# Second block of a two-block transformer: sums of a double norm made earlier, a small projection with its weights loaded, an MLP norm beside the output products

## The reference

```python
    h = rmsnorm(h, final_g)          # end of the first model, eps 1e-5
    return h[:, N_META:]
...
    h = rmsnorm_2(x, norm_mix[l])    # start of the second, eps 1e-6
    (dn_qkv, dn_z, dn_b, dn_a, ns_q, ...) = jnp.split(h @ w_in[l], splits, axis=-1)
...
    x = x + mix @ w_out[l]
    h2 = rmsnorm_2(x, norm_mlp[l])
    x = x + jnp.square(jax.nn.relu(h2 @ w_up[l])) @ w_down[l]
```

## Time and profile before

| | us |
|---|---|
| median of 3 runs | 2912.18 |
| lowest, highest | 2909.5, 2913.94 |
| the profiled execution | 2919.71 |
| its span, first to last instruction | 2917.8 |
| PE busy | 2648.9 (91%) |
| POOL busy | 1276.2 (44%) |
| DVE busy | 1204.6 (41%) |
| ACT busy | 980.7 (34%) |
| mean granted clock of PE | 0.941 |

### The profile page before, as it was taken

The page is one execution under the profiler, slowest core; times in us unless marked ns, Lnnn a source line. Parts: engine busy times, 40 slices in busy tenths (PEclk is TensorE's granted clock), DMA queues, the critical chain, the costliest instruction groups (busy, mean ns, idle before and its releaser), DMA issues.

```text
span 2917.8 us, 47590 instructions
## 1 busy us (share of the span) xinstructions
PE 2648.9 (91%) x18844; PEld 2372.1 (81%) x18844; DVE 1204.6 (41%) x1962; ACT 980.7 (34%) x1822; POOL 1276.2 (44%) x602
## 2 busy tenths in 40 slices
PE   5988999998896999999599898899999889699999
PEld 5976999998894999999588687688777777578777
DVE  5965532233776443033448543202555612220210
ACT  3335322223234332222436322233656642221221
POOL 4471665566463366566624310123111155464452
PEclk8988999999897899999789899999999989799999
DMA  4210222222220022221213000322111143132222
GB/s 134 73 59 10 79 86 76 98 75 94 66 84 15 30 96 80 96 88 64 81 44 116 16 2 2 92 67 64 47 43 44 44 154 99 43 101 87 86 87 72
DMA packets 174121, 203.88 MB, mean 70 GB/s; under 512 B 6427, under 2 KB 158582, under 8 KB 173702
## 3 DMA queue, kind: packets, MB, share of 16 engines
q1 hardware_dynamic: 170192, 199.37, 20.8%
q10 hardware_dynamic: 3766, 2.25, 0.3%
HBM read 193.22 MB, written 8.39 MB: 69 GB/s over the span
## 4 chain that ended last, share of the span: by engine, by line
PE 78%; DVE 8%; POOL 4%; issue 4%; ACT 3%; DVEq 2%; DMA 1%; ACTq 0%; POOLq 0%; SPq 0%
PE ps L716 17%; PE ps L717 16%; PE ps L718 16%; PE ps L1551 6%; POOL wlo L2742 2%; PE ps L1441 2%; PE ps L822 2%; PE ps L961 2%; PE ps L1423 1%; DVE conv L2242 1%; DVE gained L2135 1%; PE ps L1386 1%; PE ps L1169 1%; PE ps L1093 1%; DMA wraw<-in_w_proj_dn 1%
## 5 line engine op out<-in xcount | busy, mean ns | idle before, releaser
L2742 POOL TENSOR_TENSOR wlo<-wraw,whi 128x2048 fp32r<-128x2048 f32 x182 | 837.8, 4604 | 1019.3 <-ACT whi L1613 1019.1
L716 PE MATMUL ps<-hn_hi,whi 128*128 128x264 f32 (+1 forms) x2752 | 894.8, 325 | 44.4 <-POOL hn_lo L2869 12.6
L717 PE MATMUL ps<-hn_lo,whi 128*128 128x264 f32 (+1 forms) x2752 | 881.8, 320 | 0.0
L718 PE MATMUL ps<-hn_hi,wlo 128*128 128x264 f32 (+1 forms) x2752 | 879.7, 320 | 0.0
L716 PEld LDWEIGHTS ps<-hn_hi,whi 128*128 128x128 f32 x2752 | 525.5, 191 | 83.7 <-issue 36.6
L718 PEld LDWEIGHTS ps<-hn_hi,wlo 128*128 128x128 f32 x2752 | 524.3, 191 | 36.6
L717 PEld LDWEIGHTS ps<-hn_lo,whi 128*128 128x128 f32 x2752 | 525.5, 191 | 32.4
L1613 ACT CAST whi<-wraw 128x2048 fp32r<-128x2048 f32 x182 | 346.2, 1902 | 587.1 <-PE ps L718 404.1
L716 PE MATMUL ps<-ff_hi,whi 128*128 128x264 f32 x704 | 201.3, 286 | 20.9 <-POOL wlo L2742 11.4
L718 PE MATMUL ps<-ff_hi,wlo 128*128 128x264 f32 x704 | 200.3, 285 | 0.0
L717 PE MATMUL ps<-ff_lo,whi 128*128 128x264 f32 x704 | 199.9, 284 | 0.0
(11 more groups left out here) (454 smaller groups left out, 4366.9 us busy)
## 6 DMA issues: line engine op xcount, KB each, us to landing
wraw<-in_w_in SPq DMA_DIRECT2D x54, 1024.0 KB, 5.1
wraw<-in_w_gate_up SPq DMA_DIRECT2D x44, 1024.0 KB, 5.0
wraw<-in_w_up SPq DMA_DIRECT2D x16, 1024.0 KB, 5.5
wraw<-in_w_down SPq DMA_DIRECT2D x16, 1024.0 KB, 4.7
wraw<-in_w_out SPq DMA_DIRECT2D x12, 1024.0 KB, 5.1
wraw<-in_w_down SPq DMA_DIRECT2D x16, 768.0 KB, 4.5
wraw<-in_w_down SPq DMA_DIRECT2D x16, 640.0 KB, 4.3
gate_dram<-gate_out SPq DMA_DIRECT2D x16, 256.0 KB, 2.1
```

The source lines that it names most:

```text
L716: nc.tensor.matmul(dst, whi[:, slot, c:c + P], rhs_hi, start=start, stop=False)
L717: nc.tensor.matmul(dst, whi[:, slot, c:c + P], rhs_lo, start=False, stop=False)
L718: return nc.tensor.matmul(dst, wlo[:, slot, c:c + P], rhs_hi, start=False, stop=stop)
L2742: nc.gpsimd.tensor_tensor(wlo[:, slot, :], wraw[:, slot, :], whi[:, slot, :].bitcast(F32), ALU.subtract).then_inc(w_split, 1)
```

## The change

- In the last down products ACT also squares gained, and DVE adds these squares into gained_sum. As gained is h times the gain of the final norm, both sums of the double norm exist at the hand-over: sum(h^2) and sum((h g)^2). norm_sums makes eight column sums; DVE works out both scales on four columns, ACT takes one root of eight, and PE spreads two sets of rows. t2 comes straight from h with the product of both gains (mix_cols); x2 is written between the t2 steps.
- The small projection has the 64 weight columns loaded and 512 tokens streaming. It and the first two fills go chunk by chunk, as chunks come. Its result is copied by ACT and turned back by four transposes after the third fill. The gates and g are made between the steps of the first fills, on ACT (small_steps) and DVE (head_gates); the matmuls of g go from behind fill 1 to behind fill 6.
- Attention loop: p_cmp is scaled and shifted on DVE and takes one exponential for four heads, in a step and signal of its own behind the window's; DVE makes its sum. The gate copy goes from ACT to DVE.
- MLP norm: squares on ACT and sums on DVE behind each output fill, four column sums, and the first two up fills go chunk by chunk.

The diff, cut:

```diff
-            def norm2(idx):
-                for i, (ready, n) in enumerate(((sq_pool, idx - M0), (sq_dve, idx + 1))):
...
+            def norm_sums(x, at):
+                for t in range(NT2):
+                    last = nc.tensor.matmul(ps[:, 6, at + t:at + t + 1], x[:, tile(t)], ones[:, 0:1], start=True, stop=True)
+                return last
...
+            norm_sums(square_sum[:, N_META:T1], 0)
+            norm_sums(gained_sum[:, N_META:T1], NT2).then_inc(sums_done, 1)
+            pe.wait_ge(rms_ready, M0 + 1)
+            spread2(rstd, 12, 4).then_inc(rows_ready, 1)
+            spread2(rstd, 8, 5).then_inc(rows_ready, 1)
...
+            for k in range(KD):
+                pe.wait_ge(hn_ready, (M0 + 1) * KD + k + 1)
+                for c in range(2):
+                    last = product(ps[:, c, :], 0, k, c, hx(hn_hi, k, 0, SEQ), hx(hn_lo, k, 0, SEQ), k == 0, k == KD - 1)
...
+                for i, (x, w) in enumerate(((hn_hi, ws_hi), (hn_lo, ws_hi), (hn_hi, ws_lo))):
+                    last = nc.tensor.matmul(ps[0:64, 7, :], w[:, 64 * k:64 * k + 64], hx(x, k, 0, SEQ),
+                                            start=(k == 0 and i == 0), stop=(k == KD - 1 and i == 2))
+            last.then_inc(small_raw_done, 1)
...
+                if c == 2:
+                    small_turned()
+                if c == 3:
+                    pe.wait_ge(x2_ready, KD)
+                if c == 6:
                     pe.wait_ge(g_ready, 1)
...
                 nc.scalar.copy(hn(hn_hi, c, 0, T1), gained[:, c % 4, :]).then_inc(hi_ready, 1)
+                if again:
+                    nc.scalar.activation(gained_sq[:, c % 2, :], gained[:, c % 4, :], ACT.Square)
                 nc.scalar.activation(sq[:, c % 2, 0:T1], h[:, c, :], ACT.Square).then_inc(sq_ready, 1)
...
+            def small_steps(c):
+                if c == 1:
+                    act.wait_ge(small_raw_done, 1)
+                    nc.scalar.copy(small_raw, ps[0:64, 7, :]).then_inc(small_copied, 1)
+                if c == 2:
...
+                    nc.scalar.activation(gates, small[:, :, 16:64], ACT.Sigmoid)
+                    nc.scalar.activation(beta, small[:, :, 0:DN_HEADS], ACT.Sigmoid).then_inc(small_act, 1)
+                if c == 3:
+                    nc.scalar.activation(a_exp[:, 0, :], head_rows[:, 0, :], ACT.Exp)
+                    act.wait_ge(a_abs_ready, 1)
...
+                if part == 2:
+                    p = p_cmp[slot][:, :, 0:N_CMP]
+                    nc.scalar.activation(p, p, ACT.Exp)
...
-            norm2(M0 + 2, lambda c: ((x2_added, c + 1), x2[:, c, :]), eps6, M0 + 2)
+            for f in range(KD):
+                act.wait_ge(x2_added, f + 1)
+                nc.scalar.activation(sq[:, f % 2, 0:SEQ], x2[:, f, :], ACT.Square).then_inc(sq_ready, 1)
+                if f % 2:
+                    follow(PN_WO + f // 2, EV_WO + f + 1)
...
+                    if again:
+                        nc.vector.tensor_tensor(gained_sum, gained_sum, gained_sq[:, c % 2, :], ALU.add)
...
             for u in range(UNITS):
+                if u:
+                    gate_copy(u - 1)
                 if u + 1 < UNITS:
                     scores_in(u + 1)
                 combine(u)
+            gate_copy(UNITS - 1)
...
             for f in range(KD):
                 dve.wait_ge(products_done, E0 + EV_WO + f + 1)
                 nc.vector.tensor_tensor(x2[:, f, :], x2[:, f, :], ps[:, f, :], ALU.add).then_inc(x2_added, 1)
+                dve.drain()
+                if f:
+                    mlp_square(f - 1)
```

More of the change, by code:

```diff
@@ L210, in hybrid_blocks @@
         o_raw = qk_raw
-        sq8 = put("sq8", [P, KD, PADT], work)
         v_at = work + 4 * KD * T1
@@ L1525, in _ @@
                 last.then_inc(products_done, 1)
-            pe.wait_ge(x2_added, KD)
-            norm2(M0 + 2)
+            pe.wait_ge(sq_dve, M0 + 2)
+            norm_sums(mlp_sum, 0).then_inc(sums_done, 1)
+            pe.wait_ge(rms_ready, M0 + 2)
+            spread2(rstd, 8, 4).then_inc(rows_ready, 1)
+            pe.wait_ge(w_split, N0 + PN_UP[0] + 3)
+            for k in range(KD):
+                pe.wait_ge(hn_ready, (M0 + 2) * KD + k + 1)
+                for f in range(2):
+                    last = product(ps[:, f, :], 0, k, f, hx(hn_hi, k, 0, SEQ), hx(hn_lo, k, 0, SEQ), k == 0, k == KD - 1)
+                    if k == KD - 1:
+                        last.then_inc(products_done, 1)
+            pe.wait_ge(w_split, N0 + PN_UP[0] + 4)
+            for f in range(2, 4):
+                pe.wait_ge(relu_sq_ready, f + 1)
+                fill(f, 1, f % 2, hn_hi, hn_lo)
             for part in range(2):
-                with pe.Fori(0, 4) as i:
+                with pe.Fori(1 - part, 4) as i:
                     for f in range(4):
-                        if part == 0 and f == 0:
-                            pe.wait_ge(hn_ready, (M0 + 3) * KD)
                         if f % 2 == 0:
@@ L2102, in _ @@
                     follow(PN_MNS + c // 2, EV_MNS + c + 1)
-            for j in range(4):
-                follow(PN_WO + j, EV_WO + 2 * j + 2)
-            norm2(M0 + 2, lambda c: ((x2_added, c + 1), x2[:, c, :]), eps6, M0 + 2)
+            for f in range(KD):
[3 more added lines that the diff above has]
+                    follow(PN_WO + f // 2, EV_WO + f + 1)
+            act.wait_ge(rstd_ready, M0 + 2)
+            nc.scalar.activation(rstd[:, 8:12], rstd[:, 0:4], ACT.Sqrt).then_inc(rms_ready, 1)
+            split2((M0 + 2) * KD)
             for part in range(2):
@@ L2456, in _ @@
-            for ch in range(2):
-                last = nc.vector.tensor_scalar(g_half[:, ch, :], g_log.rearrange(flat), halves[:, ch:ch + 1], None, ALU.mult)
-            last.then_inc(g_ready, 1)
             nc.vector.memset(state, 0.0).then_inc(state_ready, 2)
@@ L2743, in lower @@
                                         ALU.subtract).then_inc(w_split, 1)
-            def add_squares(idx, n):
-                for c in range(1, KD // 2):
-                    pool.wait_ge(sq_ready, idx * KD + (c + 1))
-                    last = nc.gpsimd.tensor_tensor(sq8[:, 0, 0:n], sq8[:, 0, 0:n], sq8[:, c, 0:n], ALU.add)
-                    if c < KD // 2 - 1:
-                        pool.drain()
-                last.then_inc(sq_pool, 1)
             def chunk_rest(at, c):
```

245 lines of the change are left out of this document (126 added, 119 removed).

## The result

| | median, us | lowest to highest (runs) | before on the same chip | ratio, 95% interval |
|---|---|---|---|---|
| the change | 2867.73 | 2860.08 to 2875.26 (4) | 2912.24 | 0.9847 [0.9827, 0.9866] |
| after_again | 2859.43 | 2858.15 to 2864.59 (5) | 2915.58 | 0.9808 [0.9776, 0.9840] |
| after_third | 2858.39 | 2855.62 to 2861.62 (5) | 2913.23 | 0.9810 [0.9787, 0.9832] |

The first row is the measurement that the forecast was made for; the other two are the same kernel on two other occasions, beside experiments. The change makes the kernel 1.5% faster in the first and 1.9% in the others, 44.5 to 56 us. The forecast was 2861 us, 2850 to 2875. (The ratios are those on record, with their 95% intervals. They are not the quotients of the two medians and differ a little from them, most for no_table_loads: 0.9815 against 0.9795.)

What follows compares the result with a forecast made beforehand. The prediction took TensorE's matmul work as the bound (78% of the chain that ended last). Its terms, 3.3 − 34.4 + 0.6 + 2.6 − 3 − 20.4 = −51.3, took 2919.7 us to 2868.4 profiled, 2861 median, range 2850 to 2875.

Steps and rivals of the forecast that it cites:

- 1. Down products: Down turns of both layers: ACT's extra Square makes PE wait 0.55 us longer six times, +3.3 us.
- 2 and 3. Norm and products at the hand-over: Hand-over to block 2: earlier norm and chunk-paced products end at 1459.1 instead of 1493.54, −34.4 us.
- 4, turning: Behind the third qkv fill: four transposes turn the small product back, about +0.6 us.
- 5, the stall: Behind the fifth qkv fill: PE waits once for ACT, which has table loads and small steps queued, +2.6 us.
- step 3: Products at the hand-over: 72 at 0.229 us each plus a restart of 2.75 us make 19.2 us.
- 6. The attention loop: Attention loop: ACT's saving ends part of PE's long waits, −5; DVE's new work costs some; together −3 us.
- 7. The MLP norm: MLP norm: sums beside the output products and chunk-paced up fills end at 2524.2 instead of 2544.55, −20.4 us.
- the low clock through the chunk-paced fills (2883): Both restarts: clock stays at its lower level while chunks pace PE, 22 us more, 2883 us; chance 0.06.
- the loop paced by DVE (2875): Attention loop: DVE's new work shows in every unit, 11 us instead of −3, 2875 us; chance 0.11.
- no overlap (2881): Hand-over and MLP norm: fills still begin after the last chunk, each place loses about 10 us, 2881 us; chance 0.03.
- the slower case: Block 2's qkv fills: low level lasts through 22 fills, which lose 121 us, 2982 us; chance 0.02.
- Larger gain (2850): Squares hide in PE's waits, ACT does not stall, the loop gives 8: 11 us more, 2850 us; chance 0.10.

Runs made afterwards that it cites:

- no_table_loads: The change with the decay's two exponentials and logarithm in block 2's qkv fills made as Squares, so decays differ from the reference; 2853.66 us, ratio 0.9815.
- mlp_only: The kernel before with only the MLP norm's part of the change; 2890.55 us, ratio 0.9916.
- late_square: The change with ACT's Squares of gained behind the whi cast in each layer's first three down turns, DVE adding them after square_sum; 2861.05 us.
- half_square: The kernel before with an extra ACT Square over 64 of 512 columns in the down turns, result unread; 2913.19 us against 2915.58, ratio 0.9992.

## Why the prediction was right

The forecast (2861 us) lies between the three medians of the change, the sum (−51.3) next to the difference of the two profiles (−52.05). By step:

1. Down products, forecast +3.3. The mechanism I gave is there, 1.9 us a layer or +3.7 in all. What the step did not have is the clock: each wait between 2.3 and 2.9 us can be followed by a stretch at 0.50 that costs 1.45 us. On A and C, the stages of the edit, the first profile shows +12.6, after_again +6.7 and after_third +9.7, so the step was too small by 9.3, 3.4 and 6.4 us. B, which holds no edited product, is +0.6 in the first and −3.3 and −3.6 in the others. Of the 9.6 us between the first profile and after_again 5.9 lie in A and C and 3.9 in B, and of the 7.1 to after_third 2.9 and 4.2. So the first median need not be the highest by this term; the other runs were not traced.

2 and 3. Norm and products at the hand-over, −34.4; 4, turning, +0.6; 5, the stall, +2.6: together −31.2. H went from 223.8 to 193.2, 191.7 and 193.0: −30.6 to −32.1. The restart at the lower level, for which step 3 had 2.75, cost 1.5 us in the first and third, and after_again had none. Inside, the norm took 11.5 us from the last sum to the first product (10.7 forecast; the row of mix_cols can account for up to 0.7 of the 0.8) and the 72 products 18.4 (19.2). The stall was 2.92 (2.6), for the reason given: without the loads, or with one fill more between, it goes. Each load was followed at once by its function here too, so the 4.1 us that the Trainium skill's rule ("ScalarE: Activation LUTs", What ACT_TABLE_LOAD costs) would have added did not come.

6. The attention loop, −3 with bounds of −8 and +8. As an edit to before it gave −4, in the change −17 us by the medians and −14.6 by the two profiles. The step counted ACT's saving at the long waits (−5; the waits went down by 6.1) and charged DVE's new work 2 us that never showed: against traces without a long low stretch L falls by 7.7. The step missed that before's loop had two low stretches behind these waits, 6.8 us, which no trace with the new loop has. They stand in the trace of before (its mean level over the loop is 0.96), but none of my groups asked what the level did there.

7. The MLP norm, −20.4: M went from 282.6 to 262.7, −19.9, and mlp_only gave −21.8.

So the sum was right by terms 2 to 5 and 7 (−51.6 together, −50.5 in the first profile) and, in the first profile, by two errors of opposite sign, the clock's share in both left out: 9.9 us too little cost over A, B and C, 11.6 us too small a gain in step 6. That they cancel is luck. In the two later jobs the gain was 56.2 and 54.8 us, 3.5 to 5 more than the sum. Of the rivals, the low clock through the chunk-paced fills (2883) fell with the row at 1458.04, the loop paced by DVE (2875) with the 7.7 us, no overlap (2881) with the first product at 1454.21, while the last t is made from 1461.05, and the slower case with the level of 1.00 from 1458 to 1493. Larger gain (2850) had three conditions: the loop nearly met its own (7.7 of 8), but ACT did stall, 2.92 us, and the Squares did not hide.

## What to carry to other kernels

A norm between two products costs PE little of its own and much in standing still: make its sums beside the products that feed it, and let the next products start with the first finished chunk. Where they then start at the low clock, work that is paced but dense can still bring the level back, as it did here at both restarts, after 3.2 and 5.9 us.

When an operation is put on the queue of an engine that PE waits for, add to the wait what the clock may take behind it. Waits of 1.6 to 2.9 us could be enough for it here. The 20 small ones in the loop lost 6.1 us in sum, and the medians moved by 4 us in one kernel and by 17 in the other.

Look at what POOL does when DVE's new operation will start. Here adds of 0.71 us took 4.6 to 5.0 us where they started inside a subtraction on POOL, and late_square, which took the Squares out of ACT's way, gained nothing.

Compare a variant with its parent on one chip and in one job. The 6.7 us that late_square seemed to give were the difference between two measurements of the parent.

## What the runs showed that I had not expected

PE's level falls to 0.50 after waits of 1.6 to 2.9 us in the middle of dense work, but not after each of them: 2.53 us in half_square was followed by a low stretch in layer 0 and by none in layer 1, and 1.59 and 1.57 us before the same products in the loop by one of 10.2 us and by none. In the down turns of all 14 traces, each of the 14 waits of 2.90 to 2.93 us for wlo was followed by a low stretch, 14 of the 44 of 2.30 to 2.40 us, and none of the 28 of 2.39 us for ff_lo ahead of them. What decides between them these runs don't show. It makes two profiles of one kernel differ by almost 10 us (2856.3 and 2865.9 of span for the change), with the largest difference, 3.9 us, in B, which no edit touched.

Squares of 0.63 us on ACT, whose results nobody reads, in the down turns of both layers made the kernel 21 us slower by the medians (2912.34 to 2933.48), of which the trace has 9 in the stages of the Squares; with 0.25 us they cost nothing that can be measured (2915.58 to 2913.19).
